# RMS norms by quarters on TensorE's column groups, and the RWKV operands from exponentials in chunks of 65

## The reference

```python
def rmsnorm(x, g):
    y = xf * lax.rsqrt(jnp.mean(xf * xf, axis=-1, keepdims=True) + NORM_EPS)
    return y * g
...
    h = rmsnorm(x, norm_mix_pre)                  # pre
    x = x + rmsnorm(mixed @ w_out, norm_mix_post) # post
    h = rmsnorm(x, norm_ffn_pre)                  # fpre
    x = x + rmsnorm((gelu(ua) * ub) @ w_down, norm_ffn_post)  # ffn
    x = x + rmsnorm(gate * e, norm_ple)           # ple
...
    h = modulate(rmsnorm_2(x, norm1_g[i]), sh1, sc1)   # t * (1 + scale) + shift
...
    w = -softplus(-(w0 + tanh(wd) @ w2)) - 0.5;  decay = exp(-exp(w))
    iclr = sigmoid(a0 + ad @ a2);  kk = heads(k * k_k)
    kk = kk / maximum(sqrt(sum(kk * kk)), 1e-12)
    k = k * (1.0 + (iclr - 1.0) * k_a)
    y = rwkv7_scan(rh, decay, kh, vh, -kk, kk * ah)
    bonus = sum(rh * kh * r_k) * vh
```

## Time and profile before

| | us |
|---|---|
| median of 3 runs (5355.7 to 5368.65) | 5363.23 |
| the profiled execution | 5369.66 |
| its span | 5368.2 |

### The profile page before, as it was taken

How to read it: one execution, slowest core, us unless ns; L and a number is a source line. 1 busy time by engine, 2 the same in 40 slices (tenths; PEclk the granted TensorE clock), 3 DMA queues, 4 the chain that set the end, 5 groups by cost and what they waited for, 6 DMA issues and landing times. The chain is left out here.

```text
span 5368.2 us, 75318 instructions
## 1 busy us (share of the span) xinstructions
PE 4653.3 (87%) x32814; PEld 3523.3 (66%) x32814; DVE 2125.2 (40%) x3061; ACT 1504.8 (28%) x2596; POOL 646.5 (12%) x459
## 2 busy tenths in 40 slices
PE   6797997799877997979899688888889999779899
PEld 4684884587655865937587426565668885447687
DVE  3536433456345346333553412336332230334323
ACT  2523231333224232312333212135221120213222
POOL 1215100011012033000110100101000000023000
PEclk9898897899989997979999889789889999879999
DMA  3131002122221320012122151000011114300222
GB/s 129 36 110 43 4 19 80 61 90 91 83 80 40 102 75 6 4 64 90 63 94 91 52 188 52 24 31 1 32 44 63 63 58 159 98 16 29 74 98 83
DMA packets 95880, 351.65 MB, mean 66 GB/s; under 512 B 9920, under 2 KB 11328, under 8 KB 94400
## 3 DMA queue, kind: packets, MB, share of 16 engines
q1 hardware_dynamic: 85824, 312.51, 17.6%
q10 hardware_dynamic: 9728, 34.32, 1.7%
HBM read 332.11 MB, written 14.68 MB: 65 GB/s over the span
## 5 line engine op out<-in xcount | busy, mean ns | idle before, releaser
L285 DVE TENSOR_TENSOR wlo<-ring,whi 128x1024 fp32r<-128x1024 f32 x494 | 605.0, 1225 | 1988.3 <-ACT whi L275 1988.1
L275 ACT CAST whi<-ring 128x1024 fp32r<-128x1024 f32 x494 | 517.6, 1048 | 2410.3 <-PE ps L325 2229.1
L322 PE MATMUL ps<-h_hi,whi 128*128 128x512 f32 x1552 | 621.7, 401 | 98.4 <-DVEq L223 36.6
L325 PE MATMUL ps<-h_hi,wlo 128*128 128x512 f32 x1552 | 611.8, 394 | 0.0
L323 PE MATMUL ps<-h_lo,whi 128*128 128x512 f32 x1552 | 610.5, 393 | 0.0
L322 PE MATMUL ps<-hm_hi,whi 128*128 128x512 f32 (+1 forms) x1408 | 506.2, 359 | 105.1 <-POOL spread L1730 66.0
L323 PE MATMUL ps<-hm_lo,whi 128*128 128x512 f32 (+1 forms) x1408 | 478.8, 356 | 0.0
L325 PE MATMUL ps<-hm_hi,wlo 128*128 128x512 f32 (+1 forms) x1408 | 420.2, 356 | 0.0
L322 PEld LDWEIGHTS ps<-h_hi,whi 128*128 128x128 f32 x1552 | 295.9, 191 | 171.4 <-issue 52.3
L322 PEld LDWEIGHTS ps<-hm_hi,whi 128*128 128x128 f32 x1408 | 268.0, 190 | 184.2 <-POOL spread L1730 66.8
L322 PE MATMUL ps<-ac_hi,whi 128*128 128x512 f32 x880 | 328.5, 373 | 28.0 <-DVE ac_lo L450 24.8
(11 more groups left out here) (356 smaller groups left out, 7868.5 us busy)
## 6 DMA issues: line engine op xcount, KB each, us to landing
ring<-in_w SPq DMA_DIRECT2D x596, 512.0 KB, 3.3
x_spill<-x ACTq DMA_DIRECT2D x2, 2048.0 KB, 7.2
h_spill<-h ACTq DMA_DIRECT2D x2, 2048.0 KB, 6.3
m_spill<-m ACTq DMA_DIRECT2D x2, 2048.0 KB, 8.4
h<-h_spill ACTq DMA_DIRECT2D x2, 2048.0 KB, 7.7
ma<-m_spill ACTq DMA_DIRECT2D x2, 2048.0 KB, 8.1
x<-x_spill ACTq DMA_DIRECT2D x2, 2048.0 KB, 13.1
x<-in_x ACTq DMA_DIRECT2D x1, 2048.0 KB, 15.8
```

What stands on the lines that cost most here:

```text
L275: self.A.copy(self.hi[k % 2][:], raw).then_inc(self.s_cut_hi.h, 1)
L285: self.V.tensor_tensor(self.lo[k % 2][:], raw, self.hi[k % 2][:].bitcast(F32), ALU.subtract).then_inc(self.s_cut_lo.h, 1)
L322: T.matmul(ps[:, b, 0:cw], hi, xh(q, c0, cw), start=q == 0, stop=False, skip_group_check=True)
L325: m = T.matmul(ps[:, b, 0:cw], lo, xh(q, c0, cw), start=False, stop=q == kt - 1, skip_group_check=True)
```

## The change

Norms. A square's sum is now four matmuls, one for each quarter of the tokens, with 32 columns of ones each, into partitions 0, 32, 64 and 96 of one PSUM bank. So the mean of 512 tokens lies on 128 partitions by 128 columns (768: by 192). ScalarE takes the root of that with epsilon as bias, VectorE its reciprocal, into the new tile `inv`. TensorE spreads it out again: for each 64 tokens one matmul whose weights are one column of the identity, repeated, picks partition 32g of `inv` and writes it to all partitions in PSUM, where the multiplies read it. `stats_act` begins with a Sqrt of one element. `norm_to` takes the subtraction of tile j-1 behind the multiply of tile j; with a shift, ScalarE adds it in the cast and VectorE in the subtraction (`scalar_tensor_tensor`), and line 392 is gone. `add_normed` gives the even tiles' additions to VectorE, the odd ones' to GpSimd. `x_added` waits for either.

Operands of the recurrence. The exponential of the sum is written from column 1 on into chunks of 65 whose column 0 is 1.0, so one tile serves both the inclusive and the exclusive decay; the subtraction (1035) and the third exponential (988) are gone. The squares of kk go to ScalarE ahead of its sigmoids, the sigmoid of the other two rows of `low` behind them. k's factor, product and bonus input move to the first loop, k's product to GpSimd, and there the bonus matmul (`pe_bonus`). In the second loop k times the inverse decay moves to VectorE, r times the decay to GpSimd. `sml` shrinks to make room for `inv`.

The core of the diff, without the lines that it removes (they stand above):

```diff
+    def stats_pe(self, b_sq, b_root, n, wd, banks, sq):
+        T, ps, w = self.T, self.ps, wd // 4
         for j in range(n):
+            T.wait_ge(self.s_sq.h, b_sq + j + 1)
+            for g in range(4):
+                m = T.matmul(ps[32 * g:32 * g + 32, banks[0], 0:w], self.c("ones_d", 32), sq(j % 2)[:, g * w:(g + 1) * w],
+                             start=j == 0, stop=j == n - 1, skip_group_check=True)
             m.then_inc(self.s_sqm.h, 1)
+        T.wait_ge(self.s_root.h, b_root + 1)
+        for g in range(4):
+            one = CONST["ident"] + 32 * g
+            pick = self.con[:, one:one + 1].to_broadcast([P, P])
+            for c0 in range(g * w, (g + 1) * w, 64):
+                m = T.matmul(ps[:, banks[c0 // S], c0 % S:c0 % S + 64], pick,
+                             self.inv[:, c0 - g * w:c0 - g * w + 64], start=True, stop=True, skip_group_check=True)
+        m.then_inc(self.s_rsq.h, 1)
+    def stats_act(self, b_sqm, n, wd, bank, src, sq, ready=None):
+        A, w = self.A, wd // 4
+        A.activation(self.sml[:, 300:301], self.c("eps", 1), ACT.Sqrt)
         for j in range(n):
             if ready:
                 ready(j)
             if j >= 2:
...
+                A.wait_ge(self.s_sqm.h, b_sqm + j - 1)
+            A.activation(sq(j % 2), src(j), ACT.Square).then_inc(self.s_sq.h, 1)
+        A.wait_ge(self.s_sqm.h, b_sqm + n)
+        A.activation(self.inv[:, 0:w], self.ps[:, bank, 0:w], ACT.Sqrt, bias=self.c("eps", 1)).then_inc(self.s_var.h, 1)
+    def stats_dve(self, b_var, wd):
+        self.V.wait_ge(self.s_var.h, b_var + 1)
+        self.V.reciprocal(self.inv[:, 0:wd // 4], self.inv[:, 0:wd // 4]).then_inc(self.s_root.h, 1)
...
+            self.stats_act(b_sqm, DT, wd, banks[0], lambda j: self.X[:, j, 0:wd], sq, ready)
             for j in range(DT):
                 A.wait_ge(self.s_normed.h, b_norm + j + 1)
+                if shift is None:
+                    i = A.copy(hi[:, j, 0:wd], dst[:, j, 0:wd])
+                else:
+                    for si, (c0, cw) in enumerate(segs):
+                        i = A.activation(hi[:, j, c0:c0 + cw], dst[:, j, c0:c0 + cw], ACT.Identity, bias=shift(j, si))
+                i.then_inc(self.s_nhi.h, 1)
+            yield
+        def lower(j):
+            V.wait_ge(self.s_nhi.h, b_hi + j + 1)
+            if shift is None:
+                i = V.tensor_tensor(lo[:, j, 0:wd], dst[:, j, 0:wd], hi[:, j, 0:wd].bitcast(F32), ALU.subtract)
+            else:
+                for si, (c0, cw) in enumerate(segs):
+                    i = V.scalar_tensor_tensor(lo[:, j, c0:c0 + cw], dst[:, j, c0:c0 + cw], shift(j, si),
+                                               hi[:, j, c0:c0 + cw].bitcast(F32), ALU.add, ALU.subtract)
+            i.then_inc(self.s_nlo.h, 1)
         def dve():
+            self.stats_dve(b_var, wd)
             V.wait_ge(self.s_rsq.h, b_rsq + 1)
             for j in range(DT):
                 for si, (c0, cw) in enumerate(segs):
                     i = V.scalar_tensor_tensor(dst[:, j, c0:c0 + cw], self.X[:, j, c0:c0 + cw], gain(j, si),
+                                               ps[:, banks[si], 0:cw], ALU.mult, ALU.mult)
                 i.then_inc(self.s_normed.h, 1)
+                if j >= 1:
+                    lower(j - 1)
+            lower(DT - 1)
             yield
         go(pe(), act(), dve())
...
+            for j in range(0, DT, 2):
+                for i in (j + 1, j):
+                    V.scalar_tensor_tensor(Z[:, i, :], Z[:, i, :], gain(i), ps[:, bank, :], ALU.mult,
+                                           ALU.mult).then_inc(self.s_zn.h, 1)
+                V.wait_ge(self.s_zn.h, b_zn + j + 2)
+                V.tensor_tensor(self.X[:, j, 0:S], self.X[:, j, 0:S], Z[:, j, :], ALU.add).then_inc(self.s_xadv.h, 1)
             yield
         def pool():
+            for j in range(1, DT, 2):
+                G.wait_ge(self.s_zn.h, b_zn + j)
                 G.tensor_tensor(self.X[:, j, 0:S], self.X[:, j, 0:S], Z[:, j, :], ALU.add).then_inc(self.s_xadd.h, 1)
             yield
         go(pe(), act(), dve(), pool())
+        return b_add, b_adv
+    def x_added(self, eng, base, j):
+        if j % 2:
+            eng.wait_ge(self.s_xadd.h, base[0] + j // 2 + 1)
+        else:
+            eng.wait_ge(self.s_xadv.h, base[1] + j // 2 + 1)
...
+        eP = [self.view(f"e_p{i}", TMP + 16 * S + i * 520, NCH, CH + 1) for i in range(2)]
+        eN = [self.view(f"e_n{i}", TMP + 16 * S + 1040 + i * S, S) for i in range(2)]
...
+        def pe_bonus(j):
+            T.wait_ge(self.s_tb.h, b_tb + j + 1)
+            if j >= 2:
+                T.wait_ge(self.s_bonv.h, b_bonv + j - 1)
+            T.matmul(ps[:, 4 + j % 2, :], self.c("blk"), tb[j % 2][:], start=True, stop=True).then_inc(self.s_bon.h, 1)
         def pe():
+            T.wait_ge(self.s_low.h, b_low + 1)
             for j, st in enumerate(steps):
                 b0 = 2 * (j % 2)
                 if j >= 2:
@@ -947,9 +982,15 @@
                 T.matmul(ps[:, b0, :], w[0:64, :], low[0:64, 0, :], start=True, stop=True)
                 T.matmul(ps[:, b0 + 1, :], w[64:128, :], low[64:128, 0, :], start=True,
                          stop=True).then_inc(self.s_raw.h, 1)
+                if j == 1:
+                    for n in range(DT):
+                        T.wait_ge(self.s_ksq.h, b_ksq + n + 1)
+                        T.matmul(ps[0:2 * DT, 6, :], self.head_rows(n), sq[n % 2][:], start=n == 0, stop=n == DT - 1,
+                                 skip_group_check=True).then_inc(self.s_ksum.h, 1)
+                if j > 1:
+                    pe_bonus(j - 2)
+            pe_bonus(DT - 2)
+            pe_bonus(DT - 1)
...
         def act():
             A.activation(low[0:64, 0, :], low[0:64, 0, :], ACT.Tanh).then_inc(self.s_low.h, 1)
+            for j in range(DT):
+                A.wait_ge(self.s_kn.h, b_kn + j + 1)
+                if j >= 2:
+                    A.wait_ge(self.s_ksum.h, b_ksum + j - 1)
+                A.activation(sq[j % 2][:], KN[:, j, :], ACT.Square).then_inc(self.s_ksq.h, 1)
             A.wait_ge(self.s_st_m.h, self.s_st_m.n)
...
+            A.activation(low[:, 1:3, :], low[:, 1:3, :], ACT.Sigmoid).then_inc(self.s_low.h, 1)
             A.wait_ge(self.s_rn1.h, b_rn1 + 1)
             A.activation(rn, rn, ACT.Sqrt).then_inc(self.s_rn2.h, 1)
+            A.wait_ge(self.s_ones.h, ones_at + 1)
             for j in range(DT):
                 i = j % 2
                 A.wait_ge(self.s_lc.h, b_lc + j + 1)
                 if j >= 2:
+                    A.wait_ge(self.s_ken.h, b_ken + j - 1)
                     A.wait_ge(self.s_pc.h, b_pc + j - 1)
+                A.activation(eP[i][:, :, 1:CH + 1], by_chunk(lc[j][:]), ACT.Exp, scale=-DECAY_C)
+                A.activation(eN[i][:], lc[j][:], ACT.Exp, scale=DECAY_C).then_inc(self.s_te.h, 1)
...
+            V.memset(eP[0][:, :, 0:1], 1.0)
+            V.memset(eP[1][:, :, 0:1], 1.0).then_inc(self.s_ones.h, 1)
             for j in range(DT):
                 V.tensor_scalar(KN[:, j, :], K[:, j, :], self.p1("k_k", j), None, ALU.mult).then_inc(self.s_kn.h, 1)
+            V.wait_ge(self.s_st_x.h, self.s_st_x.n)
+            self.vdone()
+            V.wait_ge(self.s_kn.h, b_kn + DT)
+            for j in range(DT):
+                V.wait_ge(self.s_ia.h, b_ia + j + 1)
+                if j >= 2:
+                    V.wait_ge(self.s_kmul.h, b_kmul + j - 1)
+                V.tensor_scalar(kf[j % 2][:], BB[:, j, :], self.p1("k_a", j), ka1[:, j:j + 1], ALU.mult,
+                                ALU.add).then_inc(self.s_kf.h, 1)
+                V.tensor_tensor_scan(lc[j][:], self.con[:, CONST["segs"]:CONST["segs"] + S], AT[:, j, :], 0.0,
                                      ALU.mult, ALU.add).then_inc(self.s_lc.h, 1)
+                V.wait_ge(self.s_kmul.h, b_kmul + j + 1)
+                if j >= 2:
+                    V.wait_ge(self.s_bon.h, b_bon + j - 1)
+                V.scalar_tensor_tensor(tb[j % 2][:], R[:, j, :], self.p1("r_k", j), K[:, j, :], ALU.mult,
+                                       ALU.mult).then_inc(self.s_tb.h, 1)
+                if j > 0:
+                    bonus(j - 1)
+                if j == 2:
+                    V.wait_ge(self.s_ksum.h, b_ksum + DT)
+                    V.tensor_scalar(rn, ps[0:2 * DT, 6, :], 1e-24, None, ALU.max).then_inc(self.s_rn1.h, 1)
             V.wait_ge(self.s_rn2.h, b_rn2 + 1)
             V.reciprocal(rn, rn).then_inc(self.s_rn.h, 1)
+            bonus(DT - 1)
             for j in range(DT):
                 i = j % 2
+                V.wait_ge(self.s_te.h, b_te + j + 1)
+                V.tensor_tensor(K[:, j, :], K[:, j, :], eN[i][:], ALU.mult)
                 V.wait_ge(self.s_kspr.h, b_kspr + j + 1)
                 V.tensor_tensor(KN[:, j, :], ps[:, i, :], KN[:, j, :], ALU.mult).then_inc(self.s_knn.h, 1)
                 V.wait_ge(self.s_knn.h, b_knn + j + 1)
```

(11 more changed lines are left out.)

138 lines of the change are left out of this document (30 added, 108 removed).

## The result

| | us | ratio to before (95% interval) |
|---|---|---|
| changed kernel, median of 4 runs (5284.07 to 5292.2) | 5287.39 | 0.9856 (0.9844 to 0.9868) |
| kernel before, median of 4 runs (5355.7 to 5368.65) | 5364.86 | |
| profiled execution of the changed kernel | 5287.55 | |

The account below looks back on a forecast made before the run. TensorE is busy 87% of the span, so only its waits can be won. Norms gain 78.6 us, operands lose 3: 75.6 off the profiled 5369.7 gives 5294.1; the median, 6.5 lower, is forecast at 5287.6, range 5258 to 5326.

Parts of the forecast that it names:

- Table load: Ahead of a norm's squares: loading Sqrt's table early costs 1.5 us on the path in ten norms, 0.2 in four others.
- Column groups: A square's sum in a norm: four quarters on groups of 32 columns overlap, eight records taking 0.25 us (half clock 0.45).
- Rival 1: Sums of the norms: only two column groups overlap, 35 us less gain, 5323 in all; chance 0.10.
- rival 3: Sums of the norms: column groups take turns at half clock, costing 132 us in all, 5420, slower; chance 0.04.
- Root, reciprocal, picks: End of a norm's factor: Sqrt 0.35 us with the hop, reciprocal 0.95 (768: 1.35), sixteen pick records 3.7 (768: 5.4).
- rival 2: Spreading the norm factor: picks run at full clock, 26 us more gain, 5261 in all; chance 0.12.
- To the first multiply: Norm from first square to first multiply by its factor: 12.2 us (10.9 without table load); 768 wide 15.8 and 14.5.
- Behind it: Norm after its first multiply: four pairs of additions at 2.75 us each, 11.0; multiplies and subtractions interleaved, 10.4 without shift.
- rival 5: After the norms: TensorE doesn't follow tile by tile, sums and halves being late on ScalarE; 22 us lost, 5310; chance 0.06.
- The spread copy: First diff norm: GpSimd's copy, 6.46 us before, takes 1.0 once VectorE is free at 19.5; TensorE restarts at 20.5.
- Recurrence operands: Stage preparing the recurrence's operands: 49.8 us to the reciprocal plus 42.3 for products, 92.1 against 90.6; 3 lost in all.
- rival 4: Operands' stage (port and strides, 12 us each) and cold TensorE after overlapped columns (5) take gains back: 5316; chance 0.08.

## Why the prediction was right, by its steps

- **Table load.** Taken at 1.5 on the path in ten norms, it was 1.40 in seven. In three it began 2.0 to 2.4 us before the first square, and ScalarE then waited 0.6 to 1.0 for VectorE, so there it cost little. That it needn't be there at all the sum didn't see; the kernel without it shows 0.8 to 1.1 a norm. By the drain that the Trainium skill (ScalarE: Activation LUTs, What ACT_TABLE_LOAD costs) adds to each switch, ten loads would, as an estimate, have cost 14 us more; in the kernel without the early root the root started 1.29 after its load began, and there is no such gap.
- **Squares.** Taken at 0.61 apart (4.9 in all), they were 0.70 apart (0.90 at 768), since ScalarE waits 0.3 for each pair of sums. The root began 6.3 us after the first square where my terms gave 5.5, and 8.1 where they gave 6.8 at 768: sized too small by 0.8 and 1.3.
- **Column groups.** Four overlap: four records start within 0.02 us, eight are 0.03 apart on average. Rival 1 (two only) and rival 3 (in turns) fall, and full-width sums cost 57 us more. By the rule of the Trainium skill (TensorE: Matmul & The Clock Gate, Part 3: Packing small matmuls — row/col tiling), weight loads that share all rows wouldn't overlap; these do: eight of them take 0.20 us together, inside the 0.42 of the first sum's record.
- **Root, reciprocal, picks.** 0.37, 0.95 (1.35) and 3.67 (5.38) against 0.35, 0.95 (1.35) and 3.7 (5.4). In thirteen norms the picks ran at a granted 0.50, so rival 2 falls. The first pre's stretch shows 1.00 with the same 3.67; that stays unexplained:

```profile
43.90:47.70 3.80, 3.67 (x16) 3.49 (x16) 0.03 (x2) 0.00 (x0) 0.00 (x0) 1.00 0.00 0
1032.60:1036.40 3.80, 3.67 (x16) 3.48 (x16) 0.05 (x1) 0.00 (x0) 0.00 (x0) 0.50 0.00 0
```

- **To the first multiply.** 12.9 with the load and 11.4 without, against 12.2 and 10.9; 15.5 at 768, against 15.8 and 14.5. Up to 1.0 too little a norm, from the squares; only where the load was hidden did I take too much, 0.3 in the first modulated norms and 0.8 in the last.
- **Behind it.** A pair of additions took 2.55 (taken: 2.75), ffn's restart came 11.1 after the first multiply (11.8), fpre's halves took 10.5 (10.8), ple's last addition ended 9.8 after the first multiply (11.0): up to 1.2 too much a norm. These two errors cancel, and that is why all norms together are within 0.6 of 78.6.
- **TensorE follows tile by tile** in the second pre, diff and gqa norms: right, rival 5 falls, and the kernel without the interleave is 8.2 slower. I had put rival 5 at 22 with the halves themselves; the order alone is 7 to 8.
- **The spread copy.** TensorE restarted 20.7 after the first multiply, taken at 20.5, for partly other reasons: the transfer took 3.4 and VectorE's cuts waited for it too, so copy and cuts began together and the copy took 2.0, not 1.0.
- **Recurrence operands.** The step that failed. The part up to the reciprocal was 49.5 (taken: 49.8). The product loop was 38.6, taken at 42.3: I let GpSimd stand still for the whole 1.2 us of VectorE's two products of a tile, on top of its own 3.8 and 0.2 of hops: 5.2 a tile, eight times. (With the lead-in of 2.9 and without the first product of 1.2 these parts give 43.3; the 42.3 was added up wrong by 1.) In the trace, GpSimd is busy 34.8 of 38.6 us. Its four operations of a tile, which there include the time they were slowed, follow each other without a stop, from one first product to the next 5.1 us in one tile and 4.2 in the next, in turn:

```profile
521.71 1.62 POOL L1086 TENSOR_TENSOR ops<-ops,e_p 128x512 f32<-128x512 f32 x1
523.27 0.66 POOL L1087 COPY sml<-e_p 128x8 f32<-128x8 f32 x1
523.90 1.26 POOL L1089 TENSOR_TENSOR ops<-kn,ops 128x512 f32<-128x512 f32 x1
525.24 1.59 POOL L1091 TENSOR_TENSOR ops<-ops,e_n 128x512 f32<-128x512 f32 x1
526.79 1.17 POOL L1086 TENSOR_TENSOR ops<-ops,e_p 128x512 f32<-128x512 f32 x1
527.91 0.19 POOL L1087 COPY sml<-e_p 128x8 f32<-128x8 f32 x1
528.06 1.25 POOL L1089 TENSOR_TENSOR ops<-kn,ops 128x512 f32<-128x512 f32 x1
...
530.95 1.62 POOL L1086 TENSOR_TENSOR ops<-ops,e_p 128x512 f32<-128x512 f32 x1
```

  The last product of a tile took 1.59 in both. The four operations that were slowed in two tiles lost 0.3 to 0.5 us each (1.62 and twice 1.59 against 1.17 to 1.26, the copy 0.66 against 0.19), 0.8 a tile where I had 1.2, so a tile took 4.6 instead of 5.2. Chunks of 65 cost nothing that can be seen: 1.17 for the product that reads them, while VectorE was idle. So rival 4 falls, and the stage gained 6.3 us where I had a loss of 3.
- **What made up for it.** The windowed attention, 6.9 us longer at a lower granted clock; the sum had no term for it, and the runs don't show whether the change has a part in it. The near hit of the total is norms that were right and two misses of opposite sign: luck.

## What to carry to other kernels

Price a step in which two engines slow each other by the busy engine's own rows (they already contain what it was slowed by), over several tiles, and don't add the other engine's time in full. A wait that the trace names is the last of several: before removing it, find what would release the engine next, here the late weight cut. In the two modulated layers removing the wait alone gave 2.9 us, moving the cuts as well 21.3. Load what is repeated or broadcast as few times as the moved width allows: eight picks of 64 columns took 3.67 us, four of 128 took 2.07.
